# Four orders in a two-block float32 kernel: a broadcast in two parts, a scaling and a gate product later, four DRAM sums behind the merge

## The chip, the cores and the metric

The kernel runs on one core of a Trainium2 chip. The metric is device time in microseconds (us); less is better. TensorE (PE) multiplies, ScalarE (ACT) and VectorE (DVE) convert and combine, GpSimd (POOL) issues accumulating DMAs and takes powers, SyncE (SP) issues the loads.

## The reference

Two transformer-like blocks, one behind the other, on x of 256 rows by 2048 columns, all in float32. The first projects x, mixes it by a gated linear attention with 4 heads (mLSTM) and a second one with 8 heads (HGRN2), projects back, and adds a gated embedding. The second projects again, mixes by spatial gating and by stick-breaking attention, merges the two by gates, and ends with a feed-forward layer of width 5632 and a gated embedding.

```
proj = u @ w_in;  ml_q, ml_k, ml_v, ml_o, ml_z, ml_i, ml_f, hg_q, hg_f, hg_i, hg_g = split(proj)
h_a = mlstm_chunkwise(q_a, k_a, v_a, i_pre, f_pre)          # decays: cumulative sums of log_sigmoid(f_pre) per head
h_b = rmsnorm(hgrn2_chunkwise(q_b, k_b, logf_b, i_b), hg_norm_w)
h   = h + concat(y_a, y_b) @ w_out;  h = h + sigmoid(rmsnorm(h) @ w_pg) * (p @ w_pe);  x = rmsnorm(h)
merged = sigmoid(g_a) * (y_a2 @ w_up_a) + sigmoid(g_b) * (y_b2 @ w_up_b);  x = x + merged @ w_o
hid = rmsnorm(x) @ w_ffn_in;  x = x + (silu(gate) * up) @ w_ffn_out
x = x + sigmoid(rmsnorm(x) @ w_ple_gate) * (p2 @ w_ple)
```

## The kernel before

**Pieces.** All weights pass through the core once, in 848 pieces of 128 x 1024 numbers, numbered g. For a piece SP loads the float32 weights into `raw` (two pieces, 1 MB, in a load), ACT rounds them to `whi` (L928 or L1177), DVE takes the rest into `wlo` (L1876 or L2556), and PE multiplies with both. ACT may start piece g when PE has finished piece g - 4. PE does its work for piece g when `whi` and, for its last third, `wlo` of g are there. A standard piece (L1359, L1364) has 12 matmuls. In between, each engine does the other work of the kernel at places that are written out as numbers of pieces: `if w == L0 + 30` stands behind the conversion of piece w in DVE's order, and so on. Nothing reorders it later.

**Stages.** Pieces 0 to 127 are the first projection (A), in which both linear attentions run; 276 to 407 are the merge, 408 to 439 the projection `w_o`, 440 to 803 the feed-forward layer.

**Seven products.** From piece 290 on, a part of the weights is multiplied by a scheme with seven products M1 to M7 instead of eight: groups c = 0, 1, 2 in the merge (M1 of c = 0 is piece 290), groups 3 to 11 in the feed-forward layer. A piece of it ("s piece", L1724, L1728) has 6 matmuls. The order in a group is M1, M2, M7, M5, then M6 and M3 mixed, M4, four pieces each, with a standard piece behind every fourth. Group 3 has M1 at pieces 458 to 461, M2 at 463 to 466, M7 at 468 to 471 and M5 at 473 to 476. Loads of half a MB or 1 MB feed them. M7 and M5 need sums of two weights blocks. These sums are made in DRAM beforehand, 48 of them, 4 for each group: SP copies 1 MB (L671), POOL adds 1 MB to the copy with an accumulating DMA (L882). M4's weights are made in SBUF by accumulating DMAs (L898).

**When the sums are made.** `SUM_AT` holds a piece number for each of the 48 sums. POOL issues sum i when PE has finished that many pieces; SP puts the copy ahead of the first load that is needed at that number or later. The sums made last, 40 to 47, are for groups 10 and 11, first needed at piece 734.

**Names for the change.** `ml_cols` is PE's work behind piece 87 in stage A: it turns rows of the mLSTM's decays into columns and then spreads the decay rows over 128 partitions, by four matmuls of `sel` (L1497) into two PSUM banks ("bc", 0 and 1). DVE reads both in `ml_weights`, behind piece 91. HGRN2 works in two halves that start at pieces 23 and 49 (`HG_START`, `L0`); at L0 + 30 DVE scales a half's output (L2251). In the same iteration stands DVE's `hg_mul` (L2018, L2026, L2027) of the other half, which makes the operands of PE's level matmuls (L1431). `u_product("uB", 2)` (L2592, L2595) takes the merge's product of a slab from PSUM; the slab ends with piece 395.

Of the kernel before, what the change touches and what calls it, by code (L numbers as in the profile page):

```python
# [39 lines left out]
S = 256  # L40
# [274 lines left out]
def two_blocks_kernel(nc, A, out):  # L315
    PLAN = Plan()
    SLABS, FIRST, S_AT = PLAN.slabs, PLAN.first, PLAN.s_at
    AUX = plan_aux()
    ctx = ExitStack()
    with ctx:  # L320
# [56 lines left out]
        hrow = sb("hrow", [4, 6, S], at=rm)  # L377
# [42 lines left out]
        sel = sb("sel", [4, 4, P], at=r1)  # L420
# [43 lines left out]
        summed = nc.dram_tensor("summed", (4 * S_GROUPS, P, 4 * COLS), F32, kind="Internal").ap()  # L464
        SUM_AT = [int(24 + SUM_STEP * i) for i in range(int(116 // SUM_STEP) + 1)] + [144 + 8 * i for i in range(7)]
        SUM_AT += [199 + int(5.4 * i) for i in (0, 1, 2, 3, 8, 9, 10, 11, 12, 13)]
        SUM_AT += [PLAN.g_plan + 1 + 4 * i for i in range(4)]
        SUM_AT += [PLAN.g_out + 11 + 6 * i for i in range(4 * S_GROUPS - len(SUM_AT))]

        acc = ctx.enter_context(nc.psum_tensor("acc", [P, 4, COLS], F32))  # L470
# [8 lines left out]
        aux_full = sem("aux_full")  # L479
# [97 lines left out]
        def slab_end(role, j, q=0):  # L577

            return SLABS[PLAN.ffn_slab[role, j, q]][-1]
# [57 lines left out]
        def bank(u, n=COLS):  # L637
            return aux[:, u % 4, 0:n]
# [185 lines left out]
        def _(pool):  # L824
# [50 lines left out]
            def add_in_dram(upto):  # L875

                while added[0] < upto:
                    i = added[0]
                    added[0] += 1
                    pool.wait_ge(piece_used, SUM_AT[i])  # L880
                    pool.wait_ge(sem(f"copied{i % 4}"), 16 * (i // 4 + 1))
                    pool.dma_start(summed[i], sum_terms(i)[1], accum_op=ALU.add, max_dma_last_dim=8192)\  # L882
                        .then_inc(sem(f"summed{i % 4}"), 16)

            for i, (name, n) in enumerate(POWS):
                add_in_dram(len([g for g in SUM_AT if g <= SUMS_UPTO.get(name, 0)]))
                if name == "qk0":

                    pool.wait_ge(sem("ws_loaded"), 16)
                    pool.affine_select(out=wsT[:, :, :], in_=wsT[:, :, :], compare_op=ALU.is_ge, fill=0.0, base=0,  # L890
                                       pattern=[[0, 8], [1, P]], channel_multiplier=-1).then_inc(sem("ws_masked"), 1)
                if name in ("ffn", "ple"):
                    for c in range(M_GROUPS) if name == "ffn" else range(M_GROUPS, S_GROUPS):
                        add_in_dram(len([g for g in SUM_AT if g < S_AT[c, "M6", 0]]))
                        for m, (what, before) in S_DMA.items():
                            for q in range(4):
                                pool.wait_ge(lo_ready, S_AT[c, before, q] + 1)
                                pool.dma_start(r1[:, q], s_weights(c, what, q), accum_op=ALU.add).then_inc(sem(f"r1_added{q}"), 16)  # L898
                if name == "ffn":
                    add_in_dram(len(SUM_AT))  # L900
                pool.wait_ge(pow_in, i + 1)
                pool.tensor_tensor(rstd[:, i, 0:n], var[:, i, 0:n], minus_half[:, 0:n], ALU.pow).then_inc(pow_out, 1)

# [418 lines left out]
        def _(pe):  # L1322
# [19 lines left out]
            def free(u):  # L1342
                if u >= 4:
                    aux_taken(pe, u - 4)
# [139 lines left out]
            def ml_cols():  # L1484
                u = AUX[("atr", 0)]
                pe.wait_ge(sem("ml_em"), 1)
                free(u)
                for x, row in ((0, 1), (1, 5)):
                    for t in range(T):
                        ins = pe.transpose(bank(u)[:, x * 8 + t * 4:x * 8 + t * 4 + 4], hrow[:, row, t * P:(t + 1) * P],  # L1490
                                           ident[0:4, 0:4])
                ins.then_inc(aux_full, 1)
                for i in range(2):
                    u = AUX[("bc", i)]
                    free(u)
                    for h in range(2):
                        ins = pe.matmul(bank(u)[:, h * S:(h + 1) * S], sel[:, 2 * i + h, :], hrow[:, 3, :], start=True, stop=True)  # L1497
                    ins.then_inc(aux_full, 1)

            def ml_scores():  # L1500
                pe.wait_ge(sem("ml_qk"), 2)
# [21 lines left out]
            for s in range(16):  # L1523
                n = FIRST["A"] + s
                for p in range(8):
                    w = s * 8 + p
                    if w == 0:
                        first_piece()
                    else:
                        if s == 0:  # L1530
                            pe.wait_ge(sem("x_lo"), p + 1)
                        piece(n, p, actA, p * PK, p == 7)
                    if p == (5 if s == 1 else 2) and s - 1 in A_TRANSPOSED:
                        tr_slab(s - 1)
                    for half, L0 in enumerate(HG_START):
                        if w == L0 - 3:
                            hg_diag(half)
                        n_level, odd = divmod(w - L0, 2)
                        if 0 <= n_level < 8 and not odd:
                            hg_level(half, n_level)  # L1540
                        if w == L0 + 18:
                            hg_flip(half)
                        if w == L0 + 20:
                            hg_pv(half)
                    if (s, p) == (9, 4):
                        ml_gates()
                    if (s, p) == (9, 7):
                        ml_gates_by_token()
                    if (s, p) == (10, 4):
                        ml_gates_tr()  # L1550
                    if (s, p) == (10, 7):
                        ml_cols()
                    if (s, p) == (11, 4):
                        ml_scores()
                    for h in range(4):
                        if w == 95 + h:
                            ml_pv(h)
                    if (s, p) == (14, 4):
                        pe.wait_ge(sem("yb_ready"), 2)
                        for i in range(4, 8):  # L1560
                            transposes(("yT", i), ob, 2 * i - 8)
                    if (s, p) == (15, 2):
                        pe.wait_ge(sem("ya_ready"), 1)
                        for i in range(2):
                            transposes(("yT", i), hA, 2 * i)
# [90 lines left out]
            for s in range(10):  # L1656
                n = FIRST["E1"] + s
                for p in range(8):
# [3 lines left out]
                    w = s * 8 + p  # L1662
# [76 lines left out]
            for kind, g, *x in PLAN.merge:  # L1739
                if kind == "s":  # L1740
                    s_piece(g, x[0], x[2], x[3])
                else:
                    n, role, j, q, p = x
# [76 lines left out]
            for kind, g, *x in PLAN.ffn:  # L1820
                if kind == "s":
                    s_piece(g, x[0], x[2], x[3])
                else:
                    n, role, j, q, p = x
# [39 lines left out]
        def _(dve):  # L1864
# [335 lines left out]
            for s in range(16):  # L2200
                for p in range(8):
                    w = s * 8 + p
# [21 lines left out]
                    for half, L0 in enumerate(HG_START):  # L2224
                        if w == L0 - (7 if half else 5):
                            hg_forget(half)
                        if w == L0 - (5 if half else 3):
                            hg_cumsum(half)
                        if w == L0 - 1:
                            hg_queries(half)  # L2230
                        if w == L0 + 1:
                            hg_diagonal(half)
                        n, odd = divmod(w - L0, 2)
                        if not odd:
                            if 0 <= n - 1 < 8:
                                hg_mul(half, n - 1)
                            if 0 <= n < 8:
                                hg_sub(half, n)
                        if odd and 0 <= n - 2 < 8:
                            hg_take(half, n - 2)  # L2240
                        if w == L0 + 21:
                            hg_flipped(half)
                        if w == L0 + 24:
                            hg_output(half)
                        if w == L0 + 27:
                            dve.wait_ge(sem("ss_hB"), half + 1)
                            variance(f"hB{half}", HG_E)
                        if w == L0 + 30:
                            powered(dve, f"hB{half}")
                            x = ob[:, :, half * 512:(half + 1) * 512].rearrange("p t (h c) -> p t h c", h=4)  # L2250
                            link(dve.tensor_tensor(x, x, per_head(f"hB{half}").unsqueeze(3).to_broadcast([P, T, 4, P]), ALU.mult))  # L2251
# [82 lines left out]
            for t, (g, n, p) in enumerate(pieces(FIRST["DP"], 8)):  # L2334
                split_lo(g)
                s = n - FIRST["D"]
# [266 lines left out]
            for kind, g, *x in PLAN.merge:  # L2603
# [24 lines left out]
                        gate_taken(PLAN.ffn_slab[role, j, 0])  # L2628
                for j in range(4):
                    for role in ("uA", "uB"):  # L2630
                        if g == slab_end(role, j) + (2 if slab_end(role, j) in PLAN.block_end else 3):
                            u_product(role, j)
                for c in range(M_GROUPS):
                    if g == S_AT[c, "M2", 3] + 3:
# [216 lines left out]
```

## Time and profile before

| | |
|---|---|
| median of 3 runs | 1894.37 us (1893.72 to 1894.42) |
| the profiled execution, its own time | 1893.05 us |
| its span in the trace | 1891.3 us |
| PE busy | 1877.2 us, 99% |
| DVE, ACT, POOL busy | 1471.8, 1140.8, 130.4 us |
| DMA | 535.95 MB, mean 283 GB/s |

PE is the bound nearly everywhere, so what a change is worth is read in the few places where PE idles or runs slowly. A matmul of 512 columns starts 0.216 us behind the one before (162.67, 162.89, 163.10), though its row says 0.38 us, since matmuls overlap. A standard piece is thus 2.59 us of PE, an s piece 1.30 us. The idle time that a row of PE shows is counted from the modelled end of the matmul before, so a gap is about 0.17 us longer than the row says. Where a piece's number is given with a time, it is counted from such rows.

### The profile page before, as it was taken

What the parts mean: (1) busy time and instruction counts of PE and PEld (TensorE: products, weight loads), DVE (VectorE), ACT (ScalarE), POOL (GpSimd) and SP (SyncE); (2) the same over time, 40 slices, a digit from 0 to 9 for tenths busy, and PEclk for the clock granted to TensorE, in tenths of its full rate; (3) what the DMA queues carried; (4) which work ended last, traced back from release to release, by engine and by line L of the source; (5) the groups of instructions that cost most, each with busy time, mean ns of one, the idle gap of its engine ahead of it and who ended that gap; (6) DMA issues with size and microseconds to landing.
All of it is one profiled execution on the core that took longest, in us unless ns stands there. A gap on an engine that the chain in (4) does not pass through costs nothing.

```text
span 1891.3 us, 23371 instructions
## 1 busy us (share of the span) xinstructions
PE 1877.2 (99%) x9018; PEld 1641.9 (87%) x9018; DVE 1471.8 (78%) x1591; ACT 1140.8 (60%) x1417; POOL 130.4 (7%) x156
## 2 busy tenths in 40 slices
PE   9999999999999999999999999999999999999998
PEld 8888888888888888888888888888888888888887
DVE  6889776655666677778888657988998999898865
ACT  7556445555566556566766455666766676666553
POOL 4000011000001100000000000000000000000000
PEclk9999999999999999999999999999999999999999
DMA  9799898999989879998797886788878887987653
GB/s 392 267 284 310 274 309 272 330 347 327 309 290 312 271 269 299 321 315 278 295 313 247 330 256 239 254 311 284 276 254 320 280 271 257 327 260 249 219 188 130
DMA packets 86815, 535.95 MB, mean 283 GB/s; under 512 B 10416, under 2 KB 11184, under 8 KB 40752
## 3 DMA queue, kind: packets, MB, share of 16 engines
q1 hardware_dynamic: 72736, 458.69, 63.3%
q0 software_dynamic: 13824, 75.50, 20.6%
q8 instruction: 72, 1.18, 0.2%
q10 hardware_dynamic: 144, 0.26, 0.0%
q14 instruction: 39, 0.32, 0.0%
HBM read 529.69 MB, written 105.38 MB: 336 GB/s over the span
## 4 chain that ended last, share of the span: by engine, by line
PE 90%; DVE 5%; DMA 3%; issue 1%; ACT 1%; POOL 0%; SPq 0%; ACTq 0%; DVEq 0%; POOLq 0%
PE acc L1359 44%; PE acc L1364 22%; PE aux L1724 12%; PE aux L1728 6%; DVE wlo L2556 2%; PE aux L1338 2%; DMA ple<-in_w_ffn_in 1%; DVE wlo L1876 1%; PE aux L1431 1%; DVE ple L2551 1%; DMA ple<-in_w_in 1%; DMA raw<-summed 1%; PE aux L1805 0%; ACT whi L928 0%; ACT whi L1177 0%
## 5 line engine op out<-in xcount | busy, mean ns | idle before, releaser
L1876 DVE TENSOR_TENSOR wlo<-raw,whi 128x1024 fp32r<-128x1024 f32 x512 | 623.8, 1226 | 296.4 <-ACT whi L928 288.4
L928 ACT ACTIVATE whi<-raw 128x1024 fp32r<-128x1024 f32 x511 | 534.0, 1054 | 449.8 <-PE acc L1364 414.1
L1359 PE MATMUL acc<-whi,actA_hi 128*128 128x512 f32 x892 | 344.0, 386 | 0.7 <-ACT whi L928 0.7
L1359 PE MATMUL acc<-whi,actA_lo 128*128 128x512 f32 x892 | 339.1, 380 | 0.0
L1359 PE MATMUL acc<-whi,actB_hi 128*128 128x512 f32 x796 | 304.5, 383 | 0.2 <-DVE actB_lo L2673 0.2
L1359 PE MATMUL acc<-whi,actB_lo 128*128 128x512 f32 x796 | 301.7, 379 | 0.0
L1177 ACT ACTIVATE whi<-ple 128x1024 fp32r<-128x1024 f32 x192 | 201.0, 1055 | 139.4 <-PE acc L1364 55.6
L2556 DVE TENSOR_TENSOR wlo<-ple,whi 128x1024 fp32r<-128x1024 f32 x192 | 230.2, 1220 | 31.3 <-ACT whi L1177 28.5
L1364 PE MATMUL acc<-wlo,actA_hi 128*128 128x512 f32 x892 | 229.1, 379 | 0.0
L1364 PE MATMUL acc<-wlo,actB_hi 128*128 128x512 f32 x796 | 204.4, 379 | 0.0
L2556 DVE TENSOR_TENSOR wlo<-raw,whi 128x1024 fp32r<-128x1024 f32 x144 | 174.2, 1220 | 30.6 <-ACT whi L1177 28.9
L1359 PEld LDWEIGHTS acc<-whi,actA_hi 128*128 128x128 f32 x892 | 169.1, 190 | 25.5 <-issue 2.0
L1177 ACT ACTIVATE whi<-raw 128x1024 fp32r<-128x1024 f32 x144 | 152.0, 1055 | 64.3 <-PE acc L1364 36.5
L1364 PEld LDWEIGHTS acc<-wlo,actA_hi 128*128 128x128 f32 x892 | 168.9, 189 | 24.2
L1359 PEld LDWEIGHTS acc<-whi,actA_lo 128*128 128x128 f32 x892 | 169.2, 190 | 23.4 <-issue 0.5
L1359 PEld LDWEIGHTS acc<-whi,actB_hi 128*128 128x128 f32 x796 | 150.5, 189 | 21.6 <-DVE actB_lo L2673 1.0
L1364 PEld LDWEIGHTS acc<-wlo,actB_hi 128*128 128x128 f32 x796 | 150.4, 189 | 21.6 <-DVE wlo L1876 0.3
L1359 PEld LDWEIGHTS acc<-whi,actB_lo 128*128 128x128 f32 x796 | 150.6, 189 | 20.6
L1724 PE MATMUL aux<-whi,actB_hi 128*128 128x512 f32 x360 | 136.8, 380 | 0.8 <-ACT whi L1177 0.8
L1724 PE MATMUL aux<-whi,actB_lo 128*128 128x512 f32 x360 | 136.4, 379 | 0.0
L1728 PE MATMUL aux<-wlo,actB_hi 128*128 128x512 f32 x360 | 107.4, 380 | 0.9 <-DVE wlo L2556 0.8
L1724 PE MATMUL aux<-whi,actA_hi 128*128 128x512 f32 x216 | 83.0, 384 | 0.0
(366 smaller groups left out, 2377.0 us busy)
## 6 DMA issues: line engine op xcount, KB each, us to landing
raw<-in_w_in SPq DMA_DIRECT2D x108, 1024.0 KB, 7.3
raw<-in_w_ffn_out SPq DMA_DIRECT2D x44, 1024.0 KB, 6.9
summed<-in_w_ffn_in POOLq DMA_DIRECT2D x36, 1024.0 KB, 11.6
raw<-in_w_ffn_in SPq DMA_DIRECT2D x72, 512.0 KB, 7.9
ple<-summed SPq DMA_DIRECT2D x24, 1024.0 KB, 4.9
raw<-summed SPq DMA_DIRECT2D x48, 512.0 KB, 5.4
ple<-in_w_ffn_in SPq DMA_DIRECT2D x18, 1024.0 KB, 6.9
ple<-in_w_ffn_in POOLq DMA_DIRECT2D x36, 512.0 KB, 9.9
```

What stands on the lines that cost most here:

```text
L928: act.activation(whi[:, g % RING], raw_piece(g), ACT.Copy).then_inc(hi_ready, 1)
L1177: act.activation(whi[:, g % RING], s_source(c, m, q), ACT.Copy).then_inc(hi_ready, 1)
L1338: ins = pe.transpose(bank(u)[:, c * S + t * P:c * S + (t + 1) * P], src[:, t, (c0 + c) * P:(c0 + c + 1) * P], ident[:, :])
L1359: pe.matmul(acc2(n)[:, t, :], act[x][:, k + c, t * P:(t + 1) * P], woven(whi, g, c), start=(p == 0 and c == 0 and x == 0), stop=False)
L1364: ins = pe.matmul(acc2(n)[:, t, :], act[0][:, k + c, t * P:(t + 1) * P], woven(wlo, g, c), start=False, stop=(last and c == PK - 1))
L1431: ins = pe.matmul(bank(u)[:, c], Kp[n % 2][:, c], Qp[n % 2][:, c], start=True, stop=True)
L1724: pe.matmul(o, lhs(x, q * PK + k), woven(whi, g, k), start=(q == 0 and k == 0 and x == 0 and not onto), stop=False, skip_group_check=onto)
L1728: ins = pe.matmul(o, lhs(0, q * PK + k), woven(wlo, g, k), start=False, stop=(q == 3 and k == PK - 1), skip_group_check=onto)
L1876: dve.tensor_tensor(wlo[:, g % RING], raw_piece(g), whi[:, g % RING].bitcast(F32), ALU.subtract)\
L2551: dve.tensor_tensor(x, x, half_slot(c, S_ADDEND[m], q), ALU.add).then_inc(sem("s_sum"), 1)
L2556: dve.tensor_tensor(wlo[:, g % RING], s_source(c, m, q), whi[:, g % RING].bitcast(F32), ALU.subtract)\
```

## The change

Four places in the order of work are changed; no instruction is added to or taken from PE, ACT or DVE, and none changes its size. The diff is whole.

```diff
-        SUM_AT += [PLAN.g_plan + 1 + 4 * i for i in range(4)]
         SUM_AT += [PLAN.g_out + 11 + 6 * i for i in range(4 * S_GROUPS - len(SUM_AT))]
...
                 if name == "ffn":
-                    add_in_dram(len(SUM_AT))
+                    add_in_dram(len([g for g in SUM_AT if g < PLAN.g_ffn]))
...
                 ins.then_inc(aux_full, 1)
-                for i in range(2):
-                    u = AUX[("bc", i)]
-                    free(u)
-                    for h in range(2):
-                        ins = pe.matmul(bank(u)[:, h * S:(h + 1) * S], sel[:, 2 * i + h, :], hrow[:, 3, :], start=True, stop=True)
-                    ins.then_inc(aux_full, 1)
+
+            def ml_rows_spread(i):
+                u = AUX[("bc", i)]
+                free(u)
+                for h in range(2):
+                    ins = pe.matmul(bank(u)[:, h * S:(h + 1) * S], sel[:, 2 * i + h, :], hrow[:, 3, :], start=True, stop=True)
+                ins.then_inc(aux_full, 1)
...
                     if (s, p) == (10, 7):
                         ml_cols()
+                        ml_rows_spread(0)
+                    if (s, p) == (11, 0):
+                        ml_rows_spread(1)
...
-                        if w == L0 + 30:
+                        if w == L0 + 31:
                             powered(dve, f"hB{half}")
...
                     for role in ("uA", "uB"):
-                        if g == slab_end(role, j) + (2 if slab_end(role, j) in PLAN.block_end else 3):
+                        last = slab_end(role, j)
+                        if g == last + (2 if last in PLAN.block_end else 5 if (role, j) == ("uB", 2) else 3):
                             u_product(role, j)
```

**The spread** now has half of its matmuls behind piece 87 and half behind piece 88. **The scaling** goes one piece back: for the first half from piece 53 to 54, for the second from 79 to 80.

On DVE, around the conversions of pieces 52 to 54 in stage A, the order was as follows (L1876 is a conversion, L2251 the scaling):

```order
L1923 TENSOR_SCALAR hg_v<-acc,rstd 128x512 x2
L1876 TENSOR_TENSOR wlo<-raw,whi 128x1024 x2
L2251 TENSOR_TENSOR hg_v<-hg_v,rstd 128x2x512
L2018 TENSOR_TENSOR hg_qd<-hg_q,hg_e 128x512
L2026 TENSOR_TENSOR hg_kd<-hg_k,hg_e 128x4x64
L2027 TENSOR_TENSOR hg_kd<-hg_k,hg_e 128x4x64
L2008 TENSOR_TENSOR hg_e<-hg_b 128x512
L2009 TENSOR_TENSOR hg_e<-hg_b 128x512
L1876 TENSOR_TENSOR wlo<-raw,whi 128x1024
L2035 COPY hg_a<-aux 128x512
```

The same place in the changed kernel (its DVE lines are 3 higher):

```order
L1926 TENSOR_SCALAR hg_v<-acc,rstd 128x512 x2
L1879 TENSOR_TENSOR wlo<-raw,whi 128x1024 x2
L2021 TENSOR_TENSOR hg_qd<-hg_q,hg_e 128x512
L2029 TENSOR_TENSOR hg_kd<-hg_k,hg_e 128x4x64
L2030 TENSOR_TENSOR hg_kd<-hg_k,hg_e 128x4x64
L2011 TENSOR_TENSOR hg_e<-hg_b 128x512
L2012 TENSOR_TENSOR hg_e<-hg_b 128x512
L1879 TENSOR_TENSOR wlo<-raw,whi 128x1024
L2254 TENSOR_TENSOR hg_v<-hg_v,rstd 128x2x512
L2038 COPY hg_a<-aux 128x512
```

The scaling has moved behind five operations of the other half and one conversion.

**The gate product** `u_product("uB", 2)` goes from piece 398 to piece 400. On DVE, at the end of the merge's last group, the order was (L2570 to L2574 take M3's results, L2592 and L2595 are the product):

```order
L2570 TENSOR_TENSOR merge_h<-gate,aux 128x512
L2571 TENSOR_TENSOR gate<-aux,gate 128x512
L2574 TENSOR_TENSOR gate<-gate,merge_h 128x512
L2556 TENSOR_TENSOR wlo<-ple,whi 128x1024
L2592 TENSOR_TENSOR merge_gate<-merge_gate,acc 128x1024
L2595 TENSOR_TENSOR gate<-gate,merge_gate 128x1024
L2556 TENSOR_TENSOR wlo<-ple,whi 128x1024
L1876 TENSOR_TENSOR wlo<-raw,whi 128x1024 x3
L2581 TENSOR_TENSOR merge_h<-merge_h,aux 128x512
```

And it is now:

```order
L2573 TENSOR_TENSOR merge_h<-gate,aux 128x512
L2574 TENSOR_TENSOR gate<-aux,gate 128x512
L2577 TENSOR_TENSOR gate<-gate,merge_h 128x512
L2559 TENSOR_TENSOR wlo<-ple,whi 128x1024 x2
L1879 TENSOR_TENSOR wlo<-raw,whi 128x1024
L2595 TENSOR_TENSOR merge_gate<-merge_gate,acc 128x1024
L2598 TENSOR_TENSOR gate<-gate,merge_gate 128x1024
L1879 TENSOR_TENSOR wlo<-raw,whi 128x1024 x2
L2584 TENSOR_TENSOR merge_h<-merge_h,aux 128x512
```

Two conversions, those of pieces 399 and 400, have moved ahead of the product.

**The sums.** Without the removed line, the entries of `SUM_AT` for sums 40 to 43 are 419, 425, 431 and 437 instead of 277, 281, 285 and 289, and those for sums 44 to 47 are 443, 449, 455 and 461 instead of 419, 425, 431 and 437. Sums 0 to 39 stay. Their DMAs go from the start of the merge to the start of the feed-forward layer, while the stage of `w_o` keeps its four. On SP, from the loads of pieces 440 on, the order was (L763 loads standard pieces, L774 group 3's M1, L788 halves of a MB, L780 its M5):

```order
L763 DMA raw<-in_w_ffn_in 128x2048 x9
L774 DMA ple<-in_w_ffn_in 128x2048 x2
L763 DMA raw<-in_w_ffn_in 128x2048
L788 DMA raw<-in_w_ffn_in 128x1024 x4
L763 DMA raw<-in_w_ffn_in 128x2048
L780 DMA ple<-summed 128x2048 x2
L788 DMA raw<-summed 128x1024 x4
```

In the changed kernel the four copies (L670) stand among them:

```order
L762 DMA raw<-in_w_ffn_in 128x2048 x2
L670 DMA summed<-in_w_ffn_in 16x16384
L762 DMA raw<-in_w_ffn_in 128x2048 x3
L670 DMA summed<-in_w_ffn_in 16x16384
L762 DMA raw<-in_w_ffn_in 128x2048 x3
L670 DMA summed<-in_w_ffn_in 16x16384
L762 DMA raw<-in_w_ffn_in 128x2048
L773 DMA ple<-in_w_ffn_in 128x2048 x2
L670 DMA summed<-in_w_ffn_in 16x16384
L762 DMA raw<-in_w_ffn_in 128x2048
L787 DMA raw<-in_w_ffn_in 128x1024 x4
```

The last copy has come to stand between group 3's first loads. A copy waits on SP for the sum made four before it, and a sum waits on POOL for its copy.

## Rows read from the trace of the kernel before

**Rows 1.** The page: busy PE, and the two DMA queues (packets, MB, share).

```profile
PE 1877.2 (99%) x9018; PEld 1641.9 (87%) x9018; DVE 1471.8 (78%) x1591; ACT 1140.8 (60%) x1417; POOL 130.4 (7%) x156
...
q1 hardware_dynamic: 72736, 458.69, 63.3%
q0 software_dynamic: 13824, 75.50, 20.6%
```

**Rows 2.** Waits of PE: in total us, times, longest.

```profile
PE aux L1452 <- DVE ml_qk L2075: 2.6, 1, 2.6
...
PE aux L1431 <- DVE hg_kd L2027: 0.7, 1, 0.7
```

**Rows 3.** Windows: stretch, us, PE busy (matmuls), granted clock, DMA share, GB/s.

```profile
276.36:279.78 3.42, 3.42 (x10) 0.50 1.04 275
```

**Rows 4.** Timeline of PE behind piece 87: start, us, line, operation.

```profile
274.14 1.97 PE L1497 MATMUL aux<-hrow,sel 4*128 4x256 f32 x8
```

**Rows 5.** Timeline of DVE from piece 53 to 55.

```profile
158.79 1.22 DVE L2251 TENSOR_TENSOR hg_v<-hg_v,rstd 128x1024 f32<-128x1024 f32 x1
...
160.99 0.42 DVE L2027 TENSOR_TENSOR hg_kd<-hg_k,hg_e 128x256 f32<-128x256 f32 x1
...
164.68 1.22 DVE L1876 TENSOR_TENSOR wlo<-raw,whi 128x1024 fp32r<-128x1024 f32 x1 [0.34 <-ACT whi L928]
...
166.77 0.42 DVE L2027 TENSOR_TENSOR hg_kd<-hg_k,hg_e 128x256 f32<-128x256 f32 x1
```

**Rows 6.** Timeline of PE: the level matmuls behind pieces 51 and 53.

```profile
161.46 1.16 PE L1431 MATMUL aux<-hg_qd,hg_kd 128*128 128x128 f32 x8 [0.75 <-DVE hg_kd L2027]
...
167.63 0.61 PE L1431 MATMUL aux<-hg_qd,hg_kd 128*128 128x128 f32 x4
```

**Rows 7.** Timeline of ACT: the first M7 piece of group 0 (piece 300).

```profile
863.26 1.06 ACT L1177 ACTIVATE whi<-raw 128x1024 fp32r<-128x1024 f32 x1 [4.64 <-DMA raw<-summed]
```

**Rows 8.** Timeline of PE: end of piece 299, end of piece 302.

```profile
862.78 1.03 PE L1364 MATMUL acc<-wlo,actB_hi 128*128 128x512 f32 x4
...
868.61 0.70 PE L1728 MATMUL aux<-wlo,merge_form_hi 128*128 128x512 f32 x2
```

**Rows 9.** DMA issues, 853 to 859 us: KB, median us to landing.

```profile
raw<-summed SPq DMA_DIRECT2D x4, 512.0 KB, 9.8
```

**Rows 10.** DMA issues, 1192 to 1199 us: the same.

```profile
raw<-summed SPq DMA_DIRECT2D x4, 512.0 KB, 5.2
```

**Rows 11.** Timeline of SP: first and last issues counted for group 0.

```profile
805.41 0.33 SPq L763 DMA_DIRECT2D raw<-in_w_up_a  x1
...
853.29 5.50 SPq L788 DMA_DIRECT2D raw<-summed  x4
```

**Rows 12.** Windows, as in rows 3: around group 0's loads, before and in group 3's.

```profile
806.00:863.00 57.00, 57.00 (x278) 1.00 1.01 332
1152.00:1169.30 17.30, 17.30 (x82) 1.00 0.34 124
1169.30:1196.00 26.70, 26.70 (x129) 1.00 0.89 340
```

**Rows 13.** The four sums of 1083 to 1132 us: from issue to landing.

```profile
DMA to landing us min/median/max: 8.6/10.2/11.3
```

**Rows 14.** Timeline of ACT: M7's first conversions of group 3 (pieces 468, 469).

```profile
1198.06 2.25 ACT L1177 ACTIVATE whi<-raw 128x1024 fp32r<-128x1024 f32 x2
```

**Rows 15.** Timeline of PE: the first matmul of piece 468.

```profile
1202.76 0.38 PE L1724 MATMUL aux<-whi,actB_hi 128*128 128x512 f32 x1
```

**Rows 16.** Timeline of DVE at pieces 398 and 399.

```profile
1024.68 1.21 DVE L2592 TENSOR_TENSOR merge_gate<-merge_gate,acc 128x1024 f32<-128x1024 f32 x1
...
1027.30 1.23 DVE L2556 TENSOR_TENSOR wlo<-ple,whi 128x1024 fp32r<-128x1024 f32 x1
```

**Rows 17.** Timeline of PE: the last two matmuls of piece 399.

```profile
1028.58 0.70 PE L1728 MATMUL aux<-wlo,actB_hi 128*128 128x512 f32 x2 [0.79 <-DVE wlo L2556]
```

**Rows 18.** Timeline of ACT: group 0's last M4 piece (323).

```profile
900.07 1.06 ACT L1177 ACTIVATE whi<-ple 128x1024 fp32r<-128x1024 f32 x1 [3.68 <-DMA ple<-in_w_in]
```

## The prediction

> **What bounds the kernel now.** I read the page first: PE is busy 99% of the span and hardware loads take 63.3%, software DMAs 20.6% of the DMA engines' time [rows 1]. So only the few places count where PE waits or runs slowly, and I looked for them in the list of PE's waits, then went through the timelines around each edit. The list holds no more than 8 us; its two longest here are 2.6 us at L1452, which the change leaves alone, and 0.7 us at L1431 [rows 2]. The windows add something that no wait tells: from 276.36 to 279.78 the granted clock is 0.50, which is 1.2 of 2.4 GHz [rows 3]. It fell right behind the spread of the decay rows, 2 us in which PE's matmuls use 4 of 128 rows [rows 4]. Three of the four edits lie beside such a place, and the fourth moves DMAs away from one, to where now nothing waits.
>
> **Scaling, piece 53 to 54.** DVE's scaling starts at 158.79 and `hg_mul` stands behind it, with its last operation ending at 160.99 + 0.42 = 161.41 [rows 5]; PE's level matmuls start at 161.46 [rows 6]. The idle time in the row is 0.75; with the 0.17 that the modelled end hides and a late first matmul it is 1.0 us. Without the scaling ahead, `hg_mul` is 1.25 us earlier, and the wait goes. What is late next is the following `hg_mul`: now it ends at 166.77 + 0.42 = 167.19 [rows 5], and PE, which takes the next level at 167.63 [rows 6], will ask at 166.63. DVE had 0.34 us of idle time ahead of the conversion at 164.68 [rows 5], and the chain of five operations that starts 1.25 us earlier has the scaling put back into it, so this one ends some 0.4 us earlier, at 166.8. About 0.15 of the 1.0 us comes back. **Term: -0.85** (bounds -1.0 and 0). The second half's scaling has nothing waiting behind it: PE is over 2 us behind DVE there. If that cover were gone it would cost at most its own 1.2 us.
>
> **Spread in two parts.** The slow clock holds for 3.42 us with 10 matmuls instead of 16 [rows 3]; half of it, 1.7 us, is lost. In two parts, the sparse stretch is some 1.3 us, then a full piece of 2.59 us, then 0.9 us. The sparse stretch ahead of the fall was 2.2 us with the transposes in front, 2 us of it the spread [rows 4]. The kernel also has a bare wait of 2.6 us at L1452 [rows 2], and the clock stays up there. So length alone does not decide it, and 1.3 us is well below both. I take the fall as gone. DVE reads the second bank only at 279.1 and it will be full at about 278.8, so nothing waits for it. **Term: -1.7** (bounds 0, and +1.7 if each part brings a fall of its own).
>
> **Product, piece 398 to 400.** DVE takes the product at 1024.68 and converts piece 399 only at 1027.30 [rows 16]; PE waits, and its last two matmuls of 399 start at 1028.58 [rows 17]. They belong 0.216 behind the fourth of the piece, at 1027.6: 0.96 us, with 0.1 behind it 1.05 us. ACT has 399 ready at 1026.07, so in the new order DVE converts it until 1027.3, in time. Next in line is piece 401: 400 is converted until 1028.4, the product takes 2.6 us, and 401 ends at 1032.25, where PE asks at 1032.56. This 0.3 us of cover is thin but holds. **Term: -1.05** (bounds -1.05 and 0).
>
> **Four sums taken from the merge.** Group 0's M7 loads were 9.8 us under way [rows 9], against 5.2 in group 3 [rows 10]. ACT waited 4.64 us for the first [rows 7]. On PE, 20 matmuls stand between the starts at 862.78 and 868.61 [rows 8], 4.32 us at 0.216; they took 5.83. That is 1.5 us, with 0.1 behind it **-1.6** (bounds -1.6 and 0). With the four sums gone these loads land 4 us earlier and the stall goes. DVE then isn't late in M6, whose conversions release the accumulating DMAs of M4. The last of them made ACT wait 3.68 us [rows 18] and PE 1.9. I take 0.8 of it as given back (bounds 0 and 1.6).
>
> **The same sums put into the feed-forward layer.** This is the largest term, and it is a tally of a queue. What a 1 MB DMA keeps the engines busy for follows from rows 1: hardware, 63.3% of 1891.3 us for 458.69 MB, 2.74 us for a load or copy (1.37 for half a MB); software, 20.6% for 75.50 MB, 5.4 us for a sum. I try it on group 0. From 805.41 to the first of the four issues at 853.29 [rows 11] SP issues nine loads of 1 MB, five halves and two copies, and four sums fall in it: 24.7 + 6.9 + 5.5 + 21.6 = 58.7 us of work, while the engines are busy throughout [rows 12]. Begun at 806.7 it ends at 865.4. ACT got the data at 863.26 [rows 7]. The tally is 2 us, 4%, too high.
> Now group 3. Until 1169.3 the engines are 34% busy, then 89% of 26.7 us, which is 23.8 us of work, and 2.9 idle [rows 12]. At 1169.3 the first group load has just been let go, a burst for which SP waited. Sums 44 to 47 are issued when PE has finished 443, 449, 455 and 461 pieces, by counting back from piece 468 [rows 15] at 1147.9, 1163.5, 1179.0 and 1191.1. Sum 44 falls into the quiet stretch. Of sum 45, the last 5.4 us of some 10 from issue to landing [rows 13] are its work, and 3.6 of them lie behind 1169.3. Sums 46 and 47 add 10.8, the last copy 2.7. So 23.8 + 17.1 = 40.9 us of work, less 4%, stand ahead of M7's first load: it is through at 1208.6 and lands near 1209. Now ACT converts it at 1198.06 [rows 14] and PE takes it at 1202.76 [rows 15]. With the data at 1209, the conversion of 1.06 us puts PE's first matmul at 1210.1, 7.3 us late; DVE's conversion behind it costs another 0.3, as in group 0. **Term: +7.6** (bounds 0, if the idle slices and the lead of 4.7 us take it all, and +10). M2's halves are delayed by up to 11 us too and would land 3 us before PE needs them, so the stall is in M7.
> An idle PE of 7 us has no row here. The nearest are the wait of 2.6 us without a fall of the clock [rows 2] and the fall behind 2 us of sparse work [rows 3, 4]. A gap nearly three times as long as the first I count as one fall, **+1.7** (bounds 0 and 3.4, two such stretches). DVE's lateness in M6 moves to this group: **+0.8** (bounds 0 and 1.6).
> The Trainium skill, "TensorE: Matmul & The Clock Gate", section "Why this matters for your kernels", says that a long idle gap between bursts of matmuls sends the clock back to the lower level. By that rule the fall is certain and the sum stands at +4.1; by the wait of 2.6 us alone it would be +2.4. The trace has the fall but no gap this long, so no run here shows it yet.
> POOL: the "ffn" power (L902) stands behind sums 40 to 43 as it stood behind 44 to 47, so the rms factors are not late. SP: each copy waits for a sum that landed over 20 us before.
>
> **The sum.** -0.85 - 1.7 - 1.05 - 1.6 - 0.8 = -6.0; +7.6 + 1.7 + 0.8 = +10.1; together +4.1. The profiled execution took 1893.05 us (span 1891.3 and 1.75 around it), so 1897.2; the median of the runs is 1.3 us above it, 1894.37, and so I say **1898.5 us**.
>
> **The rivals.**
> *A, the forecast*, chance 0.50: gains of 6 and a stall of 7 to 8 us in group 3's M7. Its own range is 1896.5 to 1902, since the clock may cost twice the 1.7.
> *B, the queue takes the sums in*, 0.15: sums and loads share the engines better than the tally says, and M7's loads land before about 1201.7, the last moment for ACT. For it speaks that the loads have 4.7 us of lead and that the last sum is issued only 1 us before the first of them; against it, that the work ahead is 17 us more while 2.9 are idle, and that group 0 behaved by the tally. The time would be 1894.37 - 6.0 = 1888.4, faster.
> *C, half of it*, 0.22: the first M7 load lands near 1205, PE waits 3 us and the clock stays up. -6.0 + 3.5 + 0.5 = -2.0: 1892.4. This turns into A where the wait passes the 2.6 us after which the clock is known to have stayed up.
> *D, A and the clock of the spread doesn't come back*, 0.13: the two parts together still bring a fall, in place of the old one. It is what happens if the fall came from the low use over both parts and the piece between. 1898.5 + 1.7 = 1900.2. For it speaks that the bare wait of 2.6 us did not bring a fall, so I can't say what did.
>
> **How the numbers follow.** 0.2% is 3.8 us, about what a measurement of this kernel can tell from no change: slower begins at 1898.2, faster ends at 1890.6. A lies on that border; with the clock's cost one-sided I give two thirds of it, 0.34, to slower and 0.16 to same. D is slower, 0.13; C is same; B is faster. Slower 0.47, same 0.38, faster 0.15. The range leaves out most of B and the far ends: 1889.5 to 1902.
>
> **What would show it.** In the changed profile: no stretch of clock 0.50 near 276; no wait at L1431; piece 399's last matmuls without a wait; no wait for `raw<-summed` near 860, where M7's loads take 5 us. In group 3, near 1195, ACT waits 8 us and more for `raw<-summed`, those loads are 12 us or more under way, PE idles 7 us and its clock is 0.50 for some time behind it. The prediction is wrong if that wait is below 3 us (then B or C), or if the copies among SP's loads stop SP itself.

## The result and the profile after

The changed kernel takes 1897.7 us (median of 10 runs, 1894.92 to 1900.61), the kernel before 1893.8 us (10 runs, 1891.86 to 1895.35). The ratio is 1.0022, 95% interval [1.0012, 1.0032]: slower by 0.2%. The profiled execution of the changed kernel took 1900.6 us (span 1898.9), one of its longest runs; that of before took 1893.05, so the two traces differ by 7.55 us where the medians differ by 3.9. The ledger below says which part of it has nothing to do with the edits.

Waits of PE in the changed kernel (what waits, for what; us in total, times, longest); compare [rows 2]:

```profile
PE aux L1727 <- ACT whi L1176: 5.9, 1, 5.9
PE aux L1451 <- DVE ml_qk L2078: 2.6, 1, 2.6
```

The wait for `hg_kd` at L1431 (now L1430) is gone from the list, and so is that for DVE's `wlo` behind piece 398. A new wait stands first, 5.9 us for ACT. These are its two sides, PE behind piece 467 and ACT's conversions of pieces 468 and 469, from the timelines (start, us, line, operation); compare [rows 14, 15]:

```profile
1200.20 1.03 PE L1363 MATMUL acc<-wlo,actA_hi 128*128 128x512 f32 x4
1207.14 0.76 PE L1727 MATMUL aux<-whi,actB_hi 128*128 128x512 f32 x1 [5.92 <-ACT whi L1176]
```

```profile
1205.94 2.26 ACT L1176 ACTIVATE whi<-raw 128x1024 fp32r<-128x1024 f32 x2 [9.48 <-DMA raw<-summed]
```

ACT had nothing to convert for 9.5 us, because group 3's M7 loads took 15.2 us from issue to landing, where they took 5.2 before [rows 10]. The DMA issues of 1190 to 1197 us (KB each, median us to landing):

```profile
raw<-summed SPq DMA_DIRECT2D x4, 512.0 KB, 15.2
summed<-in_w_ffn_in POOLq DMA_DIRECT2D x1, 1024.0 KB, 12.6
```

The windows (stretch, us, busy time of PE, PEld, DVE, ACT and POOL with the numbers of their instructions, granted clock, DMA share, GB/s) show how the queue came to that, and two stretches at the lower level, 1.2 GHz:

```profile
222.77:226.18 3.41, 3.41 (x13) 2.87 (x12) 3.19 (x7) 0.00 (x0) 0.00 (x0) 0.50 0.84 168
1169.30:1200.50 31.20, 31.20 (x150) 27.33 (x149) 23.83 (x22) 16.69 (x18) 1.63 (x2) 1.00 1.02 343
1205.80:1212.63 6.83, 5.49 (x13) 4.39 (x14) 5.60 (x6) 5.18 (x5) 0.00 (x0) 0.50 1.00 402
```

From 1169.3 on the DMA share is 1.02, so the engines have no idle time to speak of, where they had 11% [rows 12]. SP was not stopped by the copies: it issues M7's loads 1.7 us earlier than before (1192.08), as much as PE is ahead by then. Its row in the changed kernel:

```profile
1190.38 6.26 SPq L787 DMA_DIRECT2D raw<-summed  x4
```

The slow stretch behind the long wait is 6.83 us long; 1.3 us of it lie in the wait itself. The other one is a surprise: it stands at 222.8, right behind the wait of 2.6 us at L1451, at which the trace of before kept the full clock. The slow stretch at 276 [rows 3] is gone.

In the merge, ACT now converts group 0's first M7 piece at 860.35 with no wait, where it waited 4.64 us [rows 7], and the second after 0.59; PE doesn't wait there at all (timeline of ACT):

```profile
860.35 1.06 ACT L1176 ACTIVATE whi<-raw 128x1024 fp32r<-128x1024 f32 x1
```

**A ledger.** I took the end of each piece on PE in both traces and looked where the difference changes; every other step is below 0.5 us, and together they come to +0.67.

| place | changed minus before, us |
|---|---|
| first 14 pieces (loads at the start; no edit near) | +1.86 |
| scaling: piece 52, and 54, 60 | -1.02, +0.46 |
| behind the wait at L1451, piece 70 (slow clock) | +1.67 |
| spread: pieces 88 and 89 | -2.55, +1.25 |
| group 0's M7: pieces 300, 302 | -1.62 |
| group 0's last M4: piece 323 | -1.14 |
| product: pieces 399, 401 | -0.69, +0.15 |
| group 3's M7: pieces 468, 469 | +8.78 |
| group 3's M4: piece 491 | -0.27 |

The lines at the edits add up to +3.35. The first line and the one of piece 70, +3.53 together, are what one execution has and another not: the other nine traces stand at -0.3 to +0.1 behind piece 13, and the fall at piece 70 is followed through all traces below.

### The profile page after: what moved, and what is told of

It reads as the page before. It is cut to its first block, busy times and chain, and to the rows that moved or that the text cites. A ratio compares the mean times of both kernels' runs of the same rounds, so it can differ in the third digit from the quotient of the medians.

```text
span 1898.9 us, 23371 instructions
## 1 busy us (share of the span) xinstructions
PE 1881.8 (99%) x9018; PEld 1645.0 (87%) x9018; DVE 1473.6 (78%) x1591; ACT 1142.1 (60%) x1417; POOL 130.1 (7%) x156
## 4 chain that ended last, share of the span: by engine, by line
PE 90%; DVE 4%; DMA 3%; issue 1%; ACT 1%; POOL 0%; SPq 0%; ACTq 0%; POOLq 0%; DVEq 0%
PE acc L1358 44%; PE acc L1363 22%; PE aux L1727 12%; PE aux L1731 6%; DVE wlo L2559 2%; PE aux L1337 2%; DMA ple<-in_w_in 1%; DMA raw<-summed 1%; PE aux L1430 1%; DVE wlo L1879 1%; DVE ple L2554 1%; DMA ple<-in_w_ffn_in 1%; PE aux L1808 0%; ACT whi L927 0%; ACT whi L1176 0%
```

## The experiments

Each ran beside the kernel before on the same chip. The stretches at clock 0.50 of all traces are compared at the end.

**Sums alone** (sums_only). The kernel before with the two lines on the sums changed.

```diff
-        SUM_AT += [PLAN.g_plan + 1 + 4 * i for i in range(4)]
...
-                    add_in_dram(len(SUM_AT))
+                    add_in_dram(len([g for g in SUM_AT if g < PLAN.g_ffn]))
```

> The kernel before with the sums moved as in the change, and nothing else. Theory (the stall in group 3's M7 is the price of the sums): the waits at pieces 300, 302 and 323 are gone (-1.6 and -1.1), PE waits some 6 us at piece 468 and runs on the slow clock behind it (+8.8 together), so about +5.8 on 1893.8: 1899.6. L1431 and piece 399 keep their waits. Rival (the three small orders changed what group 3 finds, and the sums alone would be hidden): below 1896, with a wait under 3 us at piece 468.

Measured: 1899.2 us (7 runs) beside 1894.76, ratio 1.0026 [1.0015, 1.0037]. The waits of PE:

```profile
PE aux L1723 <- ACT whi L1176: 5.6, 1, 5.6
...
PE aux L1727 <- DVE wlo L2555: 0.8, 1, 0.8
...
PE aux L1430 <- DVE hg_kd L2026: 0.7, 1, 0.7
```

The new wait is there with its size, and the two that belong to the scaling and the product have stayed. In the ledger: -1.62 in M7 and -1.42 at 323 of group 0, +7.23 at piece 468. The sums alone make the kernel slower, by 4.4 us where 5.8 were expected; the size of the stall was expected at 8.8 and came as 7.2.

**The three other orders alone** (three_orders). The changed kernel with the removed line put back (and `len(SUM_AT)` with it).

> The changed kernel with its sums where they were before (277 to 289 and 419 to 437). Theory: the wait at piece 468 is absent and those at 300, 302 and 323 are back; the three orders bring -0.7 at piece 52, -0.6 at 399, and at the spread between +0.4 (its second part is 0.4 dearer, no clock gained) and -1.3 (the slow clock gone): 1890.8 to 1893. Rival (the clock falls at one of the sparse places of stage A in every execution, wherever the spread stands): no gain from the spread, so 1892.9, and the granted clock shows 0.50 once between 210 and 290 us.

Measured: 1890.87 us (11 runs) beside 1894.76, ratio 0.9987 [0.9979, 0.9996]: faster. No wait at piece 468; the M7 waits of group 0 are back:

```profile
PE aux L1728 <- ACT whi L1177: 1.0, 2, 0.7
```

The ledger has -1.02 and +0.47 at the scaling, -2.55 and +1.25 at the spread, -0.81 and +0.15 at the product, together -2.5, which is also what the ratio gives (the medians differ by 3.9). The granted clock of this trace is 1.00 all through until the kernel's last 4 us, against the rival, which had it fall in every execution. The trace is one of the four fastest of the eleven executions, all with a mean clock of 1.000; the others list 0.999 and, at 1893.82 us, 0.998, which is more time at 0.50 than the end of any trace shows. So this kernel has falls too, in some executions.

**Which sums** (early_two, late_two). Two kernels with the changed orders, each with only two sums in the stretch before group 3's M7 and the other two behind it, at pieces 510 and 548. early_two keeps 443 and 449, late_two keeps 455 and 461.

```diff
-        SUM_AT += [PLAN.g_out + 11 + 6 * i for i in range(4 * S_GROUPS - len(SUM_AT))]
+        SUM_AT += [PLAN.g_out + 11 + 6 * i for i in range(6)] + [S_AT[c, "M1", 0] + 14 for c in (4, 5)]
```

> The changed kernel with sums 46 and 47 taken from pieces 455 and 461 to M1 + 14 of groups 4 and 5 (510, 548), 44 and 45 left at 443 and 449. Theory (a tally of the queue's work): 16 us less work ahead of group 3's first M7 load, which lands 5 to 8 us after its issue; no wait at piece 468, no slow clock, so the changed kernel less 8.8 plus at most 1.5 for the sums in groups 4 and 5: 1889 to 1890.5. Rival (too many DMAs anywhere in these 50 pieces, so 44 and 45 still cost): a wait of 2 us and more at 468.

Measured: 1890.93 us (11 runs) beside 1894.76, ratio 0.9980 [0.9971, 0.9989]. No wait at piece 468: the first M7 load lands 5.4 us behind its issue. The time is 0.4 us above the range expected. The ledger has +1.60 at piece 567, the end of group 5's M4, where ACT waits for an accumulating DMA. I put it down to the sum at 548, but not all of it can be: traces without a sum near there have up to +1.07 at that piece (holes_whole).

```diff
-        SUM_AT += [PLAN.g_out + 11 + 6 * i for i in range(4 * S_GROUPS - len(SUM_AT))]
+        SUM_AT += [PLAN.g_out + 11 + 6 * i for i in (0, 1, 2, 3, 6, 7)] + [S_AT[c, "M1", 0] + 14 for c in (4, 5)]
```

> The changed kernel with only two sums ahead of group 3, at 455 and 461, the last two places, and the other two at 510 and 548. Theory (tally): of the work ahead of the first M7 load only the late part of one sum is gone, 3.6 us (its copy and the sum at 443 ran while the engines were idle), so that load lands 3.6 us earlier and PE waits 2.4 instead of 6.1 us, with a slow clock of half the length or none: 1892 to 1894.5. Rival 1 (only the last DMAs issued before the loads matter): the wait stays at 6 us, about 1898. Rival 2 (the number of sums decides, two fewer are enough): no wait, 1889 to 1890.5, like the kernel with the early two.

Measured: 1896.04 us (11 runs) beside 1894.76, ratio 1.0010 [1.0001, 1.0019]. PE waits 4.2 us at piece 468 (5.7 with one of 1.4 in group 5), and group 3's M7 loads take this long (DMA issues, 1186.5 to 1193.5 us):

```profile
raw<-summed SPq DMA_DIRECT2D x4, 512.0 KB, 13.9
```

Two sums as well, but at the end of the stretch, and most of the stall is back: it isn't their number. The tally was too generous to the sum at 449, though: I took 3.6 us of it as work behind 1169.3. The first M1 load of group 3, issued into that backlog, took 7.3 us in the changed kernel and 4.7 here, so the backlog was 2.6 us, and the first M7 load gained 1.7 (15.5 to 13.9 us), as PE's wait did (5.9 to 4.2). The remaining 0.9 us is open. The time is above the range expected, for this and for what group 5 has here, +0.75 at piece 547 and +2.08 at 567; how much of that is the sum at 548 is as open as above.

**The dose** (half_sums, small_sums). Sums 46 and 47 add fewer of their 128 rows; the copies, the waits and the number of DMAs stay. So both kernels leave out a part of the weights' sums for group 11's M5.

```diff
+                    n = 64 if i in (46, 47) else P
-                    pool.dma_start(summed[i], sum_terms(i)[1], accum_op=ALU.add, max_dma_last_dim=8192)\
+                    pool.dma_start(summed[i][0:n], sum_terms(i)[1][0:n], accum_op=ALU.add, max_dma_last_dim=8192)\
```

> The changed kernel with sums 46 and 47 adding only 64 of 128 rows. Theory: 5.4 us less work ahead; the first M7 load lands about 10 instead of 15.5 us after its issue, and PE waits 0.7 instead of 6.1 us at piece 468. Rival 1 (copies): 4 us and more. Rival 2 (a sum costs by its issue, not by its bytes): 6 us.

> The changed kernel with sums 46 and 47 adding only 8 of 128 rows (so groups 11's M5 gets unsummed weights); their copies, waits and number of issues stay. Theory (work in the queue adds up, 5.4 us for a sum): 10.1 us less ahead of the first M7 load of group 3, which lands 5 to 7 us after its issue; no wait at piece 468. Rival (the copies, which stand in SP's own queue ahead of the loads, make them late): a wait of 4 us and more there.

Measured, one run each: 1891.61 us with 64 rows, 1889.26 with 8. The same M7 loads, with 64 rows (DMA issues, 1188 to 1195 us):

```profile
raw<-summed SPq DMA_DIRECT2D x4, 512.0 KB, 10.1
```

and with 8 rows (1189 to 1196 us):

```profile
raw<-summed SPq DMA_DIRECT2D x4, 512.0 KB, 6.3
summed<-in_w_ffn_in POOLq DMA_DIRECT2D x1, 64.0 KB, 5.7
```

PE's wait in the kernel with 64 rows:

```profile
PE aux L1728 <- ACT whi L1177: 0.4, 1, 0.4
```

Read together, that is a dose: 128 rows each, 15.2 us and a wait of 5.9; 64 rows, 10.1 and 0.4; 8 rows, 6.3 and none. From 128 to 64 rows half of two sums is taken away, which is one sum in all, for 5.1 us of queue, against 5.4 in the tally. The step from 64 to 8 rows takes away seven eighths of a sum for 3.8 us, 4.3 for a whole one: less, and the runs don't say why; the loads are then near the 5.2 us of before [rows 10], below which there is little to gain. The copies, which SP issues among its loads, are the same in all three, and with 8 rows the loads take only 1.1 us more than before. That rules the copies out as the cause of the stall; what counts is the bytes that the accumulating DMAs move ahead of the loads.

**Where the queue has room** (holes_two, holes_three). The traces of before show 53% and 58% DMA share in two stretches (windows):

```profile
646.00:658.00 12.00, 12.00 (x62) 10.56 (x60) 6.75 (x7) 6.79 (x13) 2.56 (x1) 1.00 0.53 174
672.00:695.00 23.00, 23.00 (x116) 20.31 (x116) 12.63 (x15) 14.98 (x13) 2.50 (x1) 1.00 0.58 206
```

They are pieces 222 to 225 and 231 to 238. I put two sums there and left six behind piece 408.

```diff
-        SUM_AT += [199 + int(5.4 * i) for i in (0, 1, 2, 3, 8, 9, 10, 11, 12, 13)]
+        SUM_AT += [199 + int(5.4 * i) for i in (0, 1, 2, 3)] + [223, 233] + [199 + int(5.4 * i) for i in (8, 9, 10, 11, 12, 13)]
```

> The changed kernel with two more sums made early, at pieces 223 and 233, where the DMA engines are 44 to 62% and 12 to 59% busy in the trace of the kernel with the three orders alone, and six instead of eight after piece 408 (419 to 449). Theory (a sum costs only where the queue has no room): no wait at 300, 302, 323 beyond 0.1 us, none at 468, and none in group 5 either: the kernel with the early two (1890.9) less its 1.6 us at piece 567, so 1888.5 to 1890, the fastest so far. Rival (the engines idle at 223 to 238 because loads there are bursts with deadlines, or POOL's powers queue behind the sums): a new wait of 1 us or more between 215 and 245, and 1891 or more.

Measured: 1888.96 us (6 runs, 1888.42 to 1890.73) beside 1894.46, ratio 0.9969 [0.9957, 0.9981]. PE has no new wait in either stretch, whose shares are now 80 and 92%:

```profile
646.00:658.00 12.00, 12.00 (x62) 10.56 (x61) 6.35 (x7) 7.16 (x15) 3.41 (x2) 1.00 0.80 298
672.00:695.00 23.00, 23.00 (x116) 20.34 (x115) 12.64 (x16) 14.59 (x13) 3.44 (x2) 1.00 0.92 330
```

and group 3's M7 loads land 4.7 us behind their issue (median of four). This is the lowest median of the study, though its ratio's interval overlaps that of early_two. Of the expectation only group 5 was off: 0.66 us came at piece 567, with no sum near. With a third sum there (223, 232 and 235) and five behind 408:

> The kernel holes_two with a third sum made early (223, 232, 235) and five after piece 408 (419 to 443). Theory (a sum costs only where the queue has no room): the places 223 to 238 hold about 15 us of idle engine time, three sums and copies are 24 us of work, but the loads there have several us of lead; ahead of group 3 the queue is a little emptier, where nothing waits any more. Nothing left to win: within 1 us of holes_two, 1889. Rival (three are too many there): a wait of over 1 us between pieces 232 and 245, and 1890 or more. Third (the sum at 449 still costs something in group 3): a gain of 1 us and more on holes_two.

Measured: 1889.81 us (9 runs) beside 1893.75, ratio 0.9979 [0.9969, 0.9989]; the two kernels can't be told apart.

**The spread whole again** (holes_whole), in the kernel with two sums in the holes.

```diff
                         ml_rows_spread(0)
-                    if (s, p) == (11, 0):
                         ml_rows_spread(1)
```

> The same kernel with the spread of the decay rows whole again, behind piece 87. Theory (the spread in two parts costs 0.4 and takes away a fall of the clock worth 1.7, which came behind the whole spread in both traces that had it, before and sums_only, and in none of the four that had it split): +1.3 on holes_two, and granted clock 0.50 within 2 us behind the spread. Rival (the fall behind the spread is as much a matter of chance as the one behind the wait at L1452, which three of six traces show): no fall in this trace, and the two times within 0.7 us of each other.

Measured: 1890.55 us (10 runs) beside 1894.46, ratio 0.9979 [0.9970, 0.9988], which is 1.6 us more than holes_two; the intervals of the two ratios overlap, so this verdict rests on the trace. Its windows show the fall behind the spread, and one behind L1451 as well:

```profile
219.67:223.08 3.41, 3.25 (x15) 3.25 (x16) 3.27 (x9) 0.00 (x0) 0.00 (x0) 0.50 1.02 211
277.69:281.11 3.42, 3.42 (x9) 2.69 (x10) 3.38 (x10) 0.00 (x0) 0.00 (x0) 0.50 1.01 271
```

**The clock over all traces.** There are eleven, all with the wait of 2.6 us at L1452 (L1451). A slow stretch of 3.41 us begins behind it in eight: the changed kernel, sums_only, early_two, holes_two, holes_three, holes_whole, small_sums, half_sums; none in before, three_orders and late_two. Behind the whole spread there is one in three of three traces (before, sums_only, holes_whole), behind the split spread in none of eight. The same kernel code up to there gives either answer at L1452; the split of the spread doesn't decide it (sums_only has both). What does is open.

## Why the prediction was right, step by step

The forecast was 1898.5 us with slower as the likeliest outcome; measured were 1897.7, in the forecast's own range of 1896.5 to 1902. That the kernel got slower is clear; whether by more than the 0.2% at which the forecast drew its line is not, since the interval of the ratio (1.0012 to 1.0032) lies on both sides. The mechanism A held: gains of some 5 us in stage A and the merge, and a stall with a slow clock in group 3's M7. By the terms:

- **Scaling, -0.85.** Measured -0.56. The wait is gone, in every trace with the new order (-1.02 at piece 52) and in none without it. What is late next came as named, the following `hg_mul`, and when it was worked out: its last operation ends at 168.61 and PE starts at 168.66, 0.19 later than it could, where 0.15 was said. But PE's eight matmuls behind such a wait take 1.16 us instead of 1.05, which makes it 0.29, and a later `hg_mul` is late in the same way at piece 60, for 0.17, which the term didn't look at. So 0.46 is given back instead of 0.15. Rows of DVE and PE in the changed kernel:

```profile
168.19 0.42 DVE L2030 TENSOR_TENSOR hg_kd<-hg_k,hg_e 128x256 f32<-128x256 f32 x1
```

```profile
168.66 1.16 PE L1430 MATMUL aux<-hg_qd,hg_kd 128*128 128x128 f32 x8
```

- **Spread, -1.7.** Measured -1.30 in all eight traces with the split. The slow stretch went. What the term left out is the second changeover, 0.4 us in all: the two parts take 2.1 us in place of 1.9 (277.27 to 278.31 and 281.09 to 282.15), the second starts 0.1 late, and the second matmul behind each part starts 0.31 behind the first instead of 0.22. "The clock stays up there", read at L1452 in one trace, was wrong: that wait is followed by a fall in eight of eleven. That length alone does not decide it is true all the same, since one and the same wait gives both answers. The conclusion, 1.3 us is short enough, came out right; of the two longer stretches on which it leaned, the wait was no support, and that is chance. The changed kernel's timeline of PE:

```profile
277.27 1.10 PE L1497 MATMUL aux<-hrow,sel 4*128 4x256 f32 x4
278.31 0.48 PE L1358 MATMUL acc<-whi,actA_hi 128*128 128x512 f32 x1
278.62 0.38 PE L1358 MATMUL acc<-whi,actA_lo 128*128 128x512 f32 x1
...
281.09 1.12 PE L1497 MATMUL aux<-hrow,sel 4*128 4x256 f32 x4
```

- **Product, -1.05.** Measured -0.54 here, and -0.49 to -1.06 at piece 399 over the nine traces with the new order, with 0.15 given back at 401 in all but one. The working moved DVE and PE forward by the same amount, but ACT's conversion of 399 waits for an accumulating DMA of M4, which doesn't follow. PE was 1.15 us earlier, ACT only 0.66 (it started at 1025.02 before). ACT's row in the changed kernel:

```profile
1024.36 1.06 ACT L1176 ACTIVATE whi<-ple 128x1024 fp32r<-128x1024 f32 x1 [3.91 <-DMA ple<-in_w_in]
```

- **Four sums out of the merge, -1.6 and -0.8.** Measured -1.62, in every trace without sums in the merge, and -1.14 (-0.7 to -1.4 in the others of these). three_orders, with its sums in the merge, also has -0.50 at piece 323, so up to half of the second figure may be no gain of the edit.
- **The same sums ahead of group 3, +7.6.** The first M7 load landed at 1205.92. PE was 1.7 us earlier by then, so in the terms of the working this is 1207.6, where the working had it land near 1209. PE's first matmul came 6.1 us late instead of 7.3 (1207.14, where 1201.06 was due, four starts of 0.216 behind 1200.20). The tally was right in its kind (half_sums, expected from it at 10 us, took 10.1) and a sum is 5.1 instead of 5.4 us; it erred most on the part of sum 45 that still stood in the queue at 1169.3: 3.6 us in the working, at most 2.6 by late_two. The 3.6 was also a slip: issued at 1163.5 and some 10 us under way, the sum would stand until 1173.5, which is 4.2 us, and the term would have been further off.
- **The clock behind the stall, +1.7.** It fell, and the slow stretch was 6.83 us long, so the term was 8.78 - 6.08 = 2.7 us. In sums_only and late_two, with waits of 5.6 and 4.2 us, the slow stretch was 3.41 us. The Trainium skill, "TensorE: Matmul & The Clock Gate", section "Why this matters for your kernels", has a long idle gap between bursts of matmuls send the clock back to the lower level; this trace agrees, for a gap of 6 us.
- **DVE late in M6, +0.8.** It didn't come: -0.27 at piece 491. The step carried group 0's chain over to group 3 without a row of group 3 for it.

With the measured sizes the edits sum to +3.35 us in the traces, -5.16 of gains and +8.51 of costs, where the forecast had -6.0 and +10.1. Seven of the eight terms are 0.3 to 1.5 us off, and that the total is within 1 us of +4.1 owes something to luck: gains and costs were both foretold too large. The medians have +3.9, the interval of the ratio +2.3 to +6.1. Rivals B and C fall with the 5.9 us; D falls with the eight traces. The ratios of the sums alone and of the three others alone, +0.26% and -0.13%, add to +0.13% beside the measured +0.22%, each known to 0.1%: they don't contradict that the parts add up, and the traces, place by place, show it.

## What to carry to other kernels

An accumulating DMA that is not urgent is priced by what stands behind it in the queue. What worked here: add up the engine time of all that is issued between the last idle moment and the transfer with a deadline, and compare it with the lead. Move such work to windows with a low DMA share, not to the place where no wait shows; a place without a wait may be full. And take a clock fall, or its absence, from several traces before a term of the sum rests on it.

## What was unexpected of the hardware

The same wait of 2.6 us at the same place of the same code was followed by 3.41 us at 1.2 GHz in eight traces and by none in three, worth 1.35 to 1.67 us where it came. Behind the 1.9 us of matmuls with 4 rows it came in three of three, while two halves of 1.05 us, a full piece apart, brought none in eight. The 0.1 us that PE loses behind such a stretch (278.31 to 278.62 instead of 0.216) is no matter of the 4 rows: behind the level matmuls, with 128 rows, it is there as well (162.37 to 162.67 in the kernel before).
